# The w stage of a two-block transformer kernel: weight halves stationary instead of activations

## The reference

```python
def peer(x, w_q, sub_keys_1, sub_keys_2, u_tab, v_tab):   # per block of 128 tokens
    q = (xb @ w_q).reshape(T, PEER_HEADS, 2, PEER_DKEY // 2)
    s1, s2 = q[..., 0, :] @ k1.T, q[..., 1, :] @ k2.T       # 128 keys each
    # top 16 of both, top 16 of their 256 sums: 8 heads x 16 experts of 16384
    g = softmax(top_s)
    h = einsum('thkd,td->thk', u_tab[idx], xb)
    a = gelu(h) * g
    return einsum('thk,thkd->td', a, v_tab[idx])
```

## Time and profile before

| | |
|---|---|
| time of the profiled execution | 1540.41 us |
| its span | 1538.6 us |
| TensorE matmul busy | 1510.0 us (98%) |
| TensorE weight load busy | 1390.0 us (90%) |
| VectorE busy | 1106.3 us (72%) |
| ScalarE busy | 766.1 us (50%) |
| GpSimd busy | 334.5 us (22%) |
| mean granted TensorE clock | 0.998 |
| HBM read | 341.92 MB, 223 GB/s over the span |

### The profile page before, as it was taken

How to read it: one execution, slowest core, us unless ns; L and a number is a source line. 1 busy time by engine, 2 the same in 40 slices (tenths; PEclk the granted TensorE clock), 3 DMA queues, 4 the chain that set the end, 5 groups by cost and what they waited for, 6 DMA issues and landing times.

```text
span 1538.6 us, 26335 instructions
## 1 busy us (share of the span) xinstructions
PE 1510.0 (98%) x10162; PEld 1390.0 (90%) x10162; DVE 1106.3 (72%) x2153; ACT 766.1 (50%) x1562; POOL 334.5 (22%) x240
## 2 busy tenths in 40 slices
PE   6999999999999999999999999999999899999998
PEld 6999997799999977899999999999999877777777
DVE  6766678767666775656768895666666588988887
ACT  7554555555545555544444113444433356666665
POOL 1111113202111120100016010222222134343331
PEclk9999999999999999999999999999999999999999
DMA  5555556445555564344554477888888889999996
GB/s 187 185 187 182 184 182 220 140 138 165 186 185 183 174 197 144 127 148 135 174 175 124 155 279 242 290 287 299 292 293 296 279 280 343 341 335 327 350 339 214
DMA packets 95851, 344.68 MB, mean 224 GB/s; under 512 B 10664, under 2 KB 11952, under 8 KB 95728
## 3 DMA queue, kind: packets, MB, share of 16 engines
q1 hardware_dynamic: 77296, 275.89, 53.4%
q0 software_dynamic: 18432, 67.12, 12.3%
HBM read 341.92 MB, written 1.05 MB: 223 GB/s over the span
## 4 chain that ended last, share of the span: by engine, by line
PE 85%; DVE 6%; DMA 3%; ACT 3%; issue 2%; POOL 1%; SPq 0%; DVEq 0%; ACTq 0%; POOLq 0%
PE ps L1002 84%; DMA RAW<-wall 3%; DVE WL L434 2%; ACT WH L606 1%; DVE YS L1521 1%; DVE HL L1521 1%; POOL FS L520 1%; DVE XT L1518 0%; DVE SS L1521 0%; DMA XT<-xt 0%; PE ps L1158 0%; ACT HH L624 0%; POOL SM L487 0%; DVE MX L1712 0%; PE ps L1177 0%
## 5 line engine op out<-in xcount | busy, mean ns | idle before, releaser
L434 DVE TENSOR_TENSOR WL<-RAW,WH 128x1024 fp32r<-128x1024 f32 x361 | 442.1, 1225 | 188.2 <-ACT WH L606 167.9
L606 ACT ACTIVATE WH<-RAW 128x1024 fp32r<-128x1024 f32 x354 | 373.0, 1055 | 257.3 <-PE ps L1002 243.3
L1002 PE MATMUL ps<-XT,RAW 128*128 128x192 f32 x2048 | 344.1, 327 | 0.1
L1002 PEld LDWEIGHTS ps<-XT,RAW 128*128 128x128 f32 x2048 | 331.5, 190 | 0.5 <-issue 0.4
L1002 PE MATMUL ps<-HH,WH 128*128 128x256 f32 x976 | 279.9, 287 | 0.3 <-DVE WL L434 0.3
L1002 PE MATMUL ps<-HL,WH 128*128 128x256 f32 x976 | 276.1, 283 | 0.0
L1002 PE MATMUL ps<-HH,WL 128*128 128x256 f32 x976 | 275.9, 283 | 0.0
L1002 PE MATMUL ps<-WH,GG 128*128 128x512 f32 x768 | 267.5, 400 | 5.0 <-DVE GG L1518 4.6
L1002 PE MATMUL ps<-WL,GG 128*128 128x512 f32 x512 | 203.8, 398 | 0.0
L1002 PEld LDWEIGHTS ps<-HH,WH 128*128 128x128 f32 x976 | 186.8, 191 | 2.9 <-issue 2.4
L1002 PEld LDWEIGHTS ps<-HL,WH 128*128 128x128 f32 x976 | 187.0, 192 | 1.0 <-issue 1.0
(11 more groups left out here) (271 smaller groups left out, 2449.3 us busy)
## 6 DMA issues: line engine op xcount, KB each, us to landing
RAW<-wall SPq DMA_DIRECT2D x510, 512.0 KB
B<-rel SPq DMA_DIRECT2D x4, 768.0 KB, 6.0
DEC<-con SPq DMA_DIRECT2D x4, 384.0 KB, 4.3
XT<-xt SPq DMA_DIRECT2D x4, 256.0 KB, 5.6
UB<-utab,IDXU POOLq DMA_INDIRECT x64
VB<-wall,IDXV POOLq DMA_INDIRECT x64, 8.1
WIN<-con SPq DMA_DIRECT2D x1, 768.0 KB, 8.6
out<-XT SPq DMA_DIRECT2D x2, 256.0 KB, 2.6
```

Of the source, the lines that this page charges most:

```text
L434: ins = eng.tensor_tensor(wl, RAW[:, b % NRAW, :], wh.bitcast(F), ALU.subtract)
L606: act.activation(halves(b)[0], RAW[:, b % NRAW, :], ACT.Copy).then_inc(s_hi, 1)
L1002: return pe.matmul(o, l, r, start=start, stop=stop, skip_group_check=True)
```

## The change

The w stage's operands change places. Each block's 1024 channels are taken as eight stationary slices of 128 (from WH and WL), and the 192 tokens' activations move. Per block there are now eight sums of three matmuls with 192 moving columns, 24 in all. GG becomes two tensors, GH and GL. The eight sums lie two to a bank in banks 0 to 3, channels on partitions and tokens on columns; so the residual enters with IDENT stationary and XT moving, without a turn and without ZERO. At the end ScalarE copies the four banks into OT (which lies in UB), TensorE turns each slice back with two transposes, and VectorE and ScalarE copy the turned banks 4 to 7 for the output.

```diff
-            GG = sb("GG", [128, 2, 448], R, ph)
+            GH, GL = sb("GH", [128, 2, ND], R, ph), sb("GL", [128, 2, ND], R, ph)
...
-            ZERO = sb("ZERO", [128, 64], F, ph)
...
+        OT = UB[:, :, :].rearrange("p j d -> p (j d)")[:, 0:KD * ND].rearrange("p (k t) -> p k t", k=KD)
...
-            for k in range(4):
-                o = slice(512 * (k % 2), 512 * (k % 2) + 512)
-                sp.wait_ge(s_xo, k + 1)
-                if k < 2:
-                    sp.dma_start(out[0, PAIRED, o], XO[0:NSP, k, :]).then_inc(d_out, 16)
-                else:
-                    sp.dma_start(out[1, :, o], XO[:, k, :]).then_inc(d_out, 16)
+            for h in range(2):
+                o = slice(512 * h, 512 * h + 512)
+                sp.wait_ge(s_xo, h + 1)
+                sp.dma_start(out[1, :, o], XO[:, 2 + h, :]).then_inc(d_out, 16)
+                sp.wait_ge(s_xe, 2 + h + 1)
+                sp.dma_start(out[0, PAIRED, o], XO[0:NSP, h, :]).then_inc(d_out, 16)
...
-            pool.memset(ZERO[:, :], 0.0).then_inc(s_zero, 1)
+            pool.wait_ge(s_pw, 6)
+            pool.memset(YS[NSP:128, :], 0.0).then_inc(s_zero, 1)
             pool.wait_ge(s_zero, 1)
-            pool.memset(YS[NSP:128, :], 0.0).then_inc(s_zero, 1)
-            pool.wait_ge(s_zero, 2)
...
-                act.activation(GG[:, c % 2, 0:64], BIG3[:, c, 0:64], ACT.Copy)
-                act.activation(GG[:, c % 2, 256:448], BIG3[:, c, :], ACT.Copy).then_inc(s_gh, 1)
+                act.activation(GH[:, c % 2, :], BIG3[:, c, :], ACT.Copy).then_inc(s_gh, 1)
...
-            for k in range(2):
-                act.wait_ge(s_acc, 12 + k + 1)
-                act.activation(UB[0:NSP, 0, 512 * k:512 * k + 512], bank[k][64:128, :], ACT.Copy).then_inc(s_mlow, 1)
+            for k in range(4):
+                if k < 3:
+                    act.wait_ge(s_acc, 12 + k + 1)
+                else:
+                    act.wait_ge(s_blk, N_BLOCKS)
+                act.activation(OT[:, 2 * k:2 * k + 2, :].rearrange("p k t -> p (k t)"), bank[k][:, 0:2 * ND], ACT.Copy).then_inc(s_ot, 1)
+            for h in range(2):
+                act.wait_ge(s_rtr, 2 + h + 1)
+                act.activation(XO[0:NSP, h, :], bank[6 + h][0:NSP, :], ACT.Copy).then_inc(s_xe, 1)
...
-            for k in (2, 3):
-                for m in range(4):
-                    mm(bank[k][:, c128(m)], XT[:, 4 * (k - 2) + m, 128:T], IDENT, m == 0, False)
-            pe.wait_ge(s_zero, 1)
-            for k in (0, 1):
-                for m in range(4):
-                    mm(bank[k][0:64, c128(m)], XT[:, 4 * k + m, PAIRED], IDENT, m == 0, False)
-                mm(bank[k][64:128, :], ZERO[:, :], XT[:, 0:2, :].rearrange("p k t -> p (k t)"), True, False)
+            def sums(k):
+                return bank[k // 2][:, ND * (k % 2):ND * (k % 2) + ND]
+
+            for k in range(KD):
+                mm(sums(k), IDENT, XT[:, k, DENSE], k % 2 == 0, False)
...
-                both, low, high = GG[:, s, 0:128], GG[:, s, 128:256], GG[:, s, 320:448]
-                for k in range(2):
-                    d = slice(512 * k, 512 * k + 512)
-                    mm(bank[k][:, :], both, wh[:, d], False, False)
-                    ins = mm(bank[k][:, :], both, wl[:, d], False, c == 127)
-                    if c == 127:
-                        ins.then_inc(s_acc, 1)
-                for k in range(2):
-                    d = slice(512 * k, 512 * k + 512)
-                    ins = mm3(bank[2 + k][:, :], high, low, wh[:, d], wl[:, d], False, c == 127)
-                    if c == 127 and k == 0:
+                for k in range(KD):
+                    ins = mm3(sums(k), wh[:, c128(k)], wl[:, c128(k)], GH[:, s, :], GL[:, s, :], False, c == 127)
+                    if c == 127 and k in (1, 3, 5):
                         ins.then_inc(s_acc, 1)
                 ins.then_inc(s_blk, 1)
+            for k in range(KD):
+                if k % 2 == 0:
+                    pe.wait_ge(s_ot, k // 2 + 1)
+                pe.transpose(bank[4 + k // 4][:, c128(k % 4)], OT[:, k, NSP:ND], IDENT)
+                ins = pe.transpose(bank[6 + k // 4][0:NSP, c128(k % 4)], OT[:, k, 0:NSP], IDENT)
+                if k % 4 == 3:
+                    ins.then_inc(s_rtr, 1)
...
-                tt(GG[:, c % 2, 64:256], BIG3[:, c, :], GG[:, c % 2, 256:448].bitcast(F), ALU.subtract).then_inc(s_gl, 1)
+                tt(GL[:, c % 2, :], BIG3[:, c, :], GH[:, c % 2, :].bitcast(F), ALU.subtract).then_inc(s_gl, 1)
...
-            for k in range(4):
-                if k < 2:
-                    dve.wait_ge(s_mlow, k + 1)
-                    tt(XO[0:NSP, k, :], bank[k][0:64, :], UB[0:NSP, 0, 512 * k:512 * k + 512], ALU.add).then_inc(s_xo, 1)
-                    continue
-                if k == 3:
-                    dve.wait_ge(s_blk, N_BLOCKS)
-                else:
-                    dve.wait_ge(s_acc, 12 + k + 1)
-                dve.tensor_copy(XO[:, k, :], bank[k][:, :]).then_inc(s_xo, 1)
+            for h in range(2):
+                dve.wait_ge(s_rtr, 2 + h + 1)
+                dve.tensor_copy(XO[:, 2 + h, :], bank[4 + h][:, :]).then_inc(s_xo, 1)
```

More of the change, by code:

```diff
@@ L402, in build @@
         d_u, d_v = ([sem(f"{n}{i}") for i in range(NGET)] for n in ("d_u", "d_v"))
-        s_zero, s_xe, s_xsp, s_xs, s_idx, s_dot, s_act, s_wgt, s_vs, s_half, s_ys, s_mlow = (sem(n) for n in (
+        s_zero, s_xe, s_xsp, s_xs, s_idx, s_dot, s_act, s_wgt, s_vs, s_half, s_ys, s_ot = (sem(n) for n in (
             "s_zero", "s_xe", "s_xsp", "s_xs", "s_idx", "s_dot", "s_act", "s_wgt", "s_vs", "s_half", "s_ys",
-            "s_mlow"))
+            "s_ot"))
         s_oh, s_pd, s_pp, s_bt, s_mm, s_mc, s_gel, s_tmg, s_xo = (sem(n) for n in (
@@ L2145, in summed @@
                     dve.wait_ge(s_xe, 2)
-                    dve.wait_ge(s_zero, 2)
+                    dve.wait_ge(s_zero, 1)
                 else:
```

## The result

The changed kernel takes 1579.74 us (median of 4 runs, 1579.53 to 1581.60); the kernel before 1539.63 (4 runs). The ratio is 1.0262, 95% interval 1.0241 to 1.0284: slower. Forecast were 1580.5 us, in a range of 1568 to 1604. The profiled execution has a span of 1577.7 us, 39.1 more than before.

What follows compares the result with a forecast made beforehand. TensorE was taken to bound the kernel, with weight loads pacing the new w stage. Main loop +40.2, residual -1.6 and tail +1.4 gave +40.0 on 1540.5 us: 1580.5 us, range 1568 to 1604.

Steps and rivals of the forecast that it cites:

- The pace of the main loop: w stage on TensorE: 24 narrow matmuls per block paced by their weight loads, 2.69 us a block instead of 2.34.
- x: Time of one 192-column fp32r matmul with its load in the w stage: 0.112 us, bounds 0.108 and 0.119.
- the lower bound of 0.108: Lowest forecast time per w-stage matmul, in us, the spacing of eight transposes; the stage would be +27.9 us.
- B: Rival: w-stage fp32r matmuls lose their fast rate when narrow, 1736 us as one record or 2235 as two; chance 0.11.
- C: Rival: w-stage loads stay hidden and columns decide, 0.0875 us per matmul, DMA then binds, 1509 us in all; chance 0.06.
- D: Rival: the sum lands by chance near zero, at about 0.099 us per w-stage matmul; chance 0.02.
- The stage: The w stage's 128 blocks: 345.6 us forecast against 305.4 before, +40.2 us.
- The stretch at the lower clock: Start of the w stage at the low clock: cost kept at 1.5 us, as before the change.
- The residual: At 801.85 us, TensorE's residual matmuls: 2.6 us instead of 4.25, so -1.6 us, or 0 if something else is late.
- The tail: After the last w-stage matmul: sixteen transposes, a copy and one more output, +1.4 us, bounds 0.5 and 3.
- L977, ZERO and the buffers: Removed ScalarE activations (32.5 us), removed ZERO wait and memset (0.15 us), VectorE's low half in its own buffer: 0 claimed.
- One sign: In the w stage of the new profile, VectorE's share and the DMA share would be down by about an eighth.

## Why the prediction was right, and where it was off

**The pace of the main loop** was the step that decided, and it held: x = 0.112 was forecast, 0.1116 measured. The row that carried it was that of plain fp32 matmuls with 64 columns, another type and width. The reason was right too. With the load halved the starts fell to 0.089, and with the moving side cut to 128 and 64 columns they stayed at 0.1116 and 0.111.

The transposes of the earlier trace rows should not have stood beside that row. In the tail above, those with 64 stationary columns come as slowly as those with 128. Their load records last 141 ns in the profile before (L1158), not the 190 that the prediction gives them:

```profile
L1158 PEld LDWEIGHTS ps<-COM,NAT 128*128 128x128 f32 x64 | 7.4, 141 | 1.5 <-issue 0.8
```

The plain fp32 record of 192 columns, scaled down to 128, gives the same time: 0.1625 x 128/192 = 0.108. So the row did not show a load's price, and that the lower bound of 0.108, with its 1568 us, lay so close to the measured pace was luck.

Of the rivals, B (fp32r loses its rate when narrow) falls with the changed kernel, and a smaller loss of that kind falls with the halved load, 0.089 at the same 192 columns. C (columns decide) falls with the changed kernel and with the runs that cut the columns. D didn't come about. The Trainium skill's rule for loads (TensorE: Matmul & The Clock Gate, LDWEIGHTS) goes by the stationary columns and not by what moves; the runs agree in that. For 128 columns its formula gives an estimate of 107 ns, 4% under the 0.1116 us measured at the full clock; at the lower level the runs have 0.213.

**The stage**: +40.2 forecast, +40.3 measured, but two of its parts missed and cancelled, which is luck. The stretch at the lower clock cost 2.7 us (26 starts in 5.61 us, where 2.90 would do), not 1.5: it lasted 5.4 us, where it was 3.4 before, which I had taken over unchanged. The pace was 0.0004 us better than x, 1.2 us over 3072 matmuls. The waits for VectorE went away as said.

**The residual**: -1.6 forecast, -1.8 measured (4.25 to 2.47 us). The w stage began another 1.1 us earlier; 0.9 of it is already there at 801 us, ahead of any changed instruction, and says nothing of the change.

**The tail**: +1.4 forecast, +1.65 measured. ScalarE's copies took 0.49 us each, three of them before the end of the stage and the fourth beside the transposes, as said. The transposes came every 0.11 us, as said.

**Off the path**: L977, ZERO and the buffers cost and gave nothing that shows. One sign came out weaker than said: VectorE's busy share fell from 0.87 to 0.80 and the DMA's from 0.90 to 0.83, by 8% each and not by an eighth.

**What the prediction lacked** is a rival for the clock. It wrote that the clock would be 1.00 and gave no reason but the row of before. The changed kernel entered its stage at the lower level and came up 5.4 us later; with 160 columns, one sixth fewer, the same program went down and stayed down, and took 310 us more. That the level came back at 192 columns, which no row of before could show, was luck. The mean granted clock of 0.996 to 0.998 says that it came back in all four executions of the changed kernel; the 160 columns ran once, so how often they stay down is open, and why is open too. Such a rival needed its price (24 x 0.213 x 128 = 654 us for the stage) and a chance.

## What to carry to other kernels

Count loads as well as columns: at the full clock a matmul with a 128-column fp32r stationary side cost about 0.112 us here with 192, 128 and 64 moving columns alike. So swapping operands to save 10% of the columns, at 24 loads instead of 10, made the stage 13% longer. Letting one load serve two moving tiles (16 loads) won it back, to 0.4% under the kernel before, and to 0.6% with the shorter end. Price an operation of a new shape by the slower of its two parts, each read from whatever row isolates it, even of another type; and check that the row isolates it, by working out what its other part would give, as the transposes' row was not. And where idle time stands ahead of a stretch whose matmuls are bound by loads, look at the granted clock of that stretch by itself, and give the idle time something to do.

## What the runs showed of the hardware that was not expected

- The level at which a stretch of load-bound matmuls (loads back to back, each slower than the moving columns) ran depended on what came before it. 128 moving columns per load: after 4.6 us of idle time 0.50 for 655 us; after an entry without the idle time 1.00 for 343 us. 64 columns: 1.00 at the entry, down after 4.7 us, 0.50 for the rest. 160 columns after 4.4 us of idle time: full for 0.5 us, then 0.50 for the rest. 192 columns after 4.6 us of idle time: 0.50 for 5.4 us, then 1.00; with 256 columns it came back after 3.5 us, with the halved load after 5.6. The Trainium skill (TensorE: Matmul & The Clock Gate, What's actually happening) says that the clock follows how busy TensorE has been; here both PE and its loads showed busy with almost no gap in these stretches with whole loads, whether they came up or stayed down, so the busy share of the profile's page doesn't tell which way it will go.
- At the lower level the load costs 0.213 us, 1.91 times its 0.1116 at the full clock, with 64, 128, 160 and 192 columns alike. With half the stationary columns and 192 moving ones the starts lay 0.160 apart there, so this price too is the load's.
- fp32r matmuls with 256 moving columns came every 0.120 us in this stage, 0.117 to 0.119 elsewhere; those with 192 came every 0.089 when the load was halved. Where they alternate with 384 columns under full loads, the next matmul also starts 0.089 after them; the runs don't show why.
